# A hybrid decoder layer: the order of convolutions, adaLN tiles and dense tiles around the chunked scan

## What is computed

```python
mod = silu(c) @ w_ada + b_ada                     # adaLN: 12 column tiles of 512
sh1, sc1, g1, sh2, sc2, g2 = split(mod, 6)
h = rmsnorm(x, norm1_g) * (1 + sc1) + sh1
q, k, v, ga, gb, z, xbc, dt = split(h @ w_in)
ya = diff_attention(q, k, v, ...)                 # 8 heads
xbc = silu(causal_depthwise_conv(xbc, conv_w, 4 taps) + conv_b)
xs, bm, cm = split(xbc)                           # 4 groups: xs 512 wide, B and C 128 wide each
y = ssd_chunked(xs * dtp, dtp * a_neg, bm, cm)    # 4 chunks of 128 tokens, a scan over the chunks
y = rmsnorm((y + xs * d_skip) * silu(z))          # per group
merged = sigmoid(ga) * (ya @ w_branch_a) + sigmoid(gb) * (y @ w_branch_b)
x = x + g1 * (merged @ w_out)
x = x + g2 * moe(rmsnorm(x, norm2_g) * (1 + sc2) + sh2)   # 64 experts, top 8, and a shared one
```

## Time and profile before

| | |
|---|---|
| median of three runs | 1998.27 us (1996.91 to 1998.37) |
| the profiled execution, its own time | 1995.61 us |
| its span in the profile | 1993.8 us |
| TensorE busy | 1622.1 us, 81% |
| VectorE busy | 1331.1 us, 67% |
| ScalarE busy | 933.7 us, 47% |
| mean granted TensorE clock over the span | 0.905 |

### The profile page before, as it was taken

How to read it: one execution, slowest core, us unless ns; L and a number is a source line. 1 busy time by engine, 2 the same in 40 slices (tenths; PEclk the granted TensorE clock), 3 DMA queues, 4 the chain that set the end, 5 groups by cost and what they waited for, 6 DMA issues and landing times.

```text
span 1993.8 us, 22702 instructions
## 1 busy us (share of the span) xinstructions
PE 1622.1 (81%) x7242; PEld 1263.5 (63%) x7243; DVE 1331.1 (67%) x1714; ACT 933.7 (47%) x1136; POOL 304.6 (15%) x298
## 2 busy tenths in 40 slices
PE   6697797689798888987878554899999789999960
PEld 1484685567676666765667443687777568877750
DVE  2487467576664656656554674788888457888849
ACT  2325424421324324243233214688887457888740
POOL 1000000011020200201010054222222122222210
PEclk9699899799998989998899776999999889999985
DMA  8021031167211112111142107899999568999948
GB/s 283 22 85 43 22 106 43 71 217 268 99 43 64 43 64 84 43 64 43 42 183 69 43 14 304 324 351 378 359 365 373 199 236 327 373 367 356 347 175 362
DMA packets 103538, 361.43 MB, mean 181 GB/s; under 512 B 19116, under 2 KB 29552, under 8 KB 76432
## 3 DMA queue, kind: packets, MB, share of 16 engines
q1 hardware_dynamic: 71472, 278.41, 37.6%
q0 software_dynamic: 27040, 62.07, 8.5%
q10 hardware_dynamic: 4928, 19.78, 2.5%
HBM read 352.18 MB, written 43.66 MB: 199 GB/s over the span
## 4 chain that ended last, share of the span: by engine, by line
PE 53%; DVE 19%; DMA 14%; ACT 6%; issue 5%; POOL 2%; SPq 0%; ACTq 0%; POOLq 0%; DVEq 0%
PE psum L1279 13%; PE psum L1280 13%; PE psum L1281 13%; DMA rawm<-in_w_exp_up 9%; DVE cv L1804 3%; PE psum L691 2%; DVE ring L850 2%; POOL slot_table L542 2%; ACT hl L1075 2%; PE psum L1301 2%; PE psum L1501 1%; DVE ofin L933 1%; DVE hl L1586 1%; ACT ring L778 1%; DVE modacc L1599 1%
## 5 line engine op out<-in xcount | busy, mean ns | idle before, releaser
L850 DVE TENSOR_TENSOR ring<-rawm,ring 128x2048 fp32r<-128x2048 f32 x192 | 436.3, 2286 | 40.0 <-ACT ring L778 39.4
L778 ACT ACTIVATE ring<-rawm 128x2048 fp32r<-128x2048 f32 x192 | 368.0, 1918 | 92.4 <-DMA rawm<-in_w_exp_up 40.9
L1279 PE MATMUL psum<-ring,xT 128*128 128x512 f32 x528 | 223.9, 424 | 26.2 <-DVE ring L850 21.4
L1586 DVE TENSOR_TENSOR hl<-raw,hl 128x2048 fp32r<-128x2048 f32 x59 | 135.1, 2292 | 137.4 <-ACT hl L1075 136.9
L1281 PE MATMUL psum<-ring,xT 128*128 128x512 f32 x528 | 210.5, 399 | 0.0
L1280 PE MATMUL psum<-ring,xT 128*128 128x512 f32 x528 | 210.4, 398 | 0.0
L1279 PE MATMUL psum<-hl,hT 128*128 128x512 f32 x416 | 164.7, 396 | 15.5 <-DVE hT L1881 11.2
L637 POOL DMA_INDIRECT y_rows<-yb,row_of x64 | 99.5, 1555 | 438.1 <-ACT yb L822 427.8
L1280 PE MATMUL psum<-hl,hT 128*128 128x512 f32 x416 | 163.6, 393 | 0.0
L1281 PE MATMUL psum<-hl,hT 128*128 128x512 f32 x416 | 163.6, 393 | 0.0
L1279 PE MATMUL psum<-hT,hl 128*128 128x512 f32 x320 | 139.3, 435 | 0.0
(11 more groups left out here) (374 smaller groups left out, 3100.3 us busy)
## 6 DMA issues: line engine op xcount, KB each, us to landing
rawm<-in_w_exp_gate SPq DMA_DIRECT2D x64, 1024.0 KB, 12.2
rawm<-in_w_exp_up SPq DMA_DIRECT2D x64, 1024.0 KB, 15.1
rawm<-in_w_exp_down SPq DMA_DIRECT2D x64, 1024.0 KB, 9.8
raw<-in_w_in SPq DMA_DIRECT2D x36, 1024.0 KB, 5.1
modraw<-in_w_ada POOLq DMA_DIRECT2D x16, 1024.0 KB, 5.7
ysum<-y_rows ACTq DMA_DIRECT2D x16, 1024.0 KB, 9.0
raw<-in_w_ada SPq DMA_DIRECT2D x8, 1024.0 KB, 9.4
raw<-in_w_branch_b SPq DMA_DIRECT2D x8, 1024.0 KB, 5.3
```

The source lines that it names most:

```text
L778: A(ring[:, slot, 1, :], rawm[slot][:], ACT.Copy).then_inc(S["m_hi2"], 1)
L850: TT(ring[:, slot, 0, :], rawm[slot][:], ring[:, slot, 1, :].bitcast(F32), ALU.subtract).then_inc(S["m_lo2"], 1)
L1279: M(dst, lhs(0), rhs(0), start=first, stop=False)
L1586: TT(hl[:, slot, 0, :], raw[slot][:], hl[:, slot, 1, :].bitcast(F32), ALU.subtract).then_inc(S["lo_done"], 1)
```

## The change

- **adaLN halves.** `modacc` has two buffers. The matmul `modp` of a tile comes two output tiles after its second half, and `take_mod` (now a step `modt`) three after. The halves start on the same dense tiles, with `bc` of group 0 now ahead of `xs` of group 0; the last four halves stand behind bc 0, bc 1, xs 0 and xs 1.
- **Convolutions.** B and C of group g+1 (q = 4, 5) are convolved behind the second tile of each of the two b bases of group g; for group 0 behind xs 2 and xs 3. Those of xs stand behind z tiles 0 (q = 0), 1 (q = 1, 2) and 2 (q = 3). `yb_hl` no longer lies over `cv` but over `xs_rows` and `lm`; the convolution of B waits instead for the state products of the group before.
- **The opening of the scan.** "rows" is cut in two: "bc" (B, C, decays of chunk 0, `b_rows`, `cbm`) stands ahead of the four z tiles, "xs" (transposes of xs, inputs of chunk 0) behind them.
- **Filling.** For groups 0 to 2: bc 0 behind "xs", bc 1 behind chunk 0, xs 0 behind chunk 1, xs 1 behind chunk 2, nothing behind chunk 3, xs 2 and xs 3 behind "last". `bc` is created ahead of `xs`. For group 3: one tile behind "xs", one behind chunk 1, two behind "last".

The core of the diff (the buffers' moves in SBUF, and the same split of "rows" on POOL and ACT, are left out):

```diff
@@ plan_steps
-    def mod_unit(j, h):
+    later = []
+
+    def mod_unit():
+        j, h = next(late)
...
-        if h == 0 and j > 4:
-            item("modp", j - 1)
         item("modu", j, u=u)
+        if h:
+            later.append([2, "modp", j])
+            later.append([3, "modt", j])
+
+    def out_mod(b, o, mod=True):
+        out(b, o)
+        for x in list(later):
+            x[0] -= 1
+            if x[0] == 0:
+                item(x[1], x[2])
+                later.remove(x)
+        if mod:
+            mod_unit()
...
-    x = xs(0)
-    for o in range(4):
-        out(x, o)
-        mod_unit(*next(late))
-    x = bc(0)
-    out(x, 0)
-    item("modp", 11)
-    out(x, 1)
+    conv = lambda g, *qs: [item("conv", g, q=q) for q in qs]
+    y, x = bc(0), xs(0)
+    for o in range(2):
+        out_mod(y, o)
+    for o in range(4):
+        out_mod(x, o, o < 2)
+        if o >= 2:
+            conv(0, 2 + o)
+    item("modt", 11)
     for g in range(G4):
         z = base("row", ("z", g), halves(w["w_in"], OZ + g * 512), 4)
-        for o, qs in enumerate(((4, 5), (0,), (1, 2), (3,))):
-            for q in qs:
-                item("conv", g, q=q)
+        part = lambda p: item("ssd", g, part=p)
+        part("bc")
+        for o in range(4):
             out(z, o)
+            conv(g, *((0,), (1, 2), (3,), ())[o])
+        part("xs")
         if g < G4 - 1:
-            x, y = xs(g + 1), bc(g + 1)
-            fill = {"rows": (x, 0), 0: (x, 1), 1: (x, 2), 2: (x, 3), 3: (y, 0), "last": (y, 1)}
+            y, x = bc(g + 1), xs(g + 1)
+            fill = {"xs": [(y, 0)], 0: [(y, 1)], 1: [(x, 0)], 2: [(x, 1)], "last": [(x, 2), (x, 3)]}
         else:
             x = base("col", ("gb", 0), halves(w["w_in"], OGB), 4)
-            fill = {"rows": (x, 0), 1: (x, 1), 3: (x, 2), "last": (x, 3)}
-        for part in ("rows", 0, 1, 2, 3, "last", "norm"):
-            item("ssd", g, part=part)
-            if part in fill:
-                out(*fill[part])
+            fill = {"xs": [(x, 0)], 1: [(x, 1)], "last": [(x, 2), (x, 3)]}
...
         for b in range(2):
-            whole(base("branch", ("b", g, b), [[(0, 512, 0, 4, cols(w["w_b"], g * 512, 4, b * 512))]], 4))
+            x = base("branch", ("b", g, b), [[(0, 512, 0, 4, cols(w["w_b"], g * 512, 4, b * 512))]], 4)
+            for o in range(4):
+                out(x, o)
+                if g < G4 - 1 and o == 1:
+                    conv(g + 1, 4 + b)
@@ TensorE
-                    M(bank(7), ones[:], modacc[:], start=True, stop=True).then_inc(S["mod_ps"], 1)
+                    M(bank(7), ones[:], modacc[:, tag % 2], start=True, stop=True).then_inc(S["mod_ps"], 1)
...
-                        else:
-                            pe.wait_ge(S["yT_lo"], HEADS + 4 * g)
                         pe.wait_ge(S["conv_silu"], 6 * g + 2)
...
                         segments(0)
+                    elif s["part"] == "xs":
                         pe.wait_ge(S["conv_silu"], 6 * (g + 1))
@@ VectorE
-                if u["half"] == 0:
-                    take_mod(u["tag"])
+                if u["half"] == 0 and u["tag"] >= 6:
+                    v.wait_ge(S["mod_ps"], u["tag"] - 1)
...
-                        v.wait_ge(S["proj_done"], out_index[("b", g - 1, 1)] + 4)
+                        v.wait_ge(S["ys_ps"], 4 * g)
```

More of the change, by code:

```diff
@@ L86, in __call__ @@
         return t
+CONV = (4, 5, 0, 1, 2, 3)
 def plan_steps(w):
@@ L151, in plan_steps @@
         for o in range(4):
-            out(x, o)
-            mod_unit(*next(late))
+            out_mod(x, o)
     item("spill", 0)
@@ L1005, in _ @@
                     g = s["tag"]
-                    ch = {"rows": 0, 0: 1, 1: 2, 2: 3, 3: 4}.get(s["part"])
+                    ch = {"bc": 0, 0: 1, 1: 2, 2: 3, 3: 4}.get(s["part"])
                     if ch is not None:
@@ L1667, in _ @@
                     mod_rows(s["u"])
+                elif kind == "modt":
+                    take_mod(tag + 1)
                 elif kind == "h":
@@ L1835, in chunk_inputs @@
                            ALU.mult).then_inc(S["m_ready"], 1)
[L1837 to L1838 removed]
+                    if s["part"] == "bc":
                         v.wait_ge(S["cb_ps"], 2 * g + 2)
```

40 lines of the change are left out of this document (21 added, 19 removed).

## The result

| | before | after |
|---|---|---|
| median | 1998.32 us (1996.91 to 2001.42, four runs) | 1971.56 us (1964.36 to 1974.21, four runs) |
| the profiled execution, its own time | 1995.61 us | 1973.67 us |
| its span | 1993.8 us | 1971.9 us |
| ratio of the times | | 0.9865, 95% interval 0.9842 to 0.9887 |

The account below looks back on a forecast made before the run. TensorE was taken as the bound, waiting on VectorE's wrongly ordered queue, with slow clock after waits. Terms -17.5 - 10.5 + 0.3 - 3 = -30.7 gave 1967 us from the 1998.3 median; range 1958 to 1978, with rivals 1956 to 1983.

Parts of the forecast that it names:

- opening of group 0, with the adaLN sums: Start of the mixer: sums -13.5, group 0's opening -5.5, slow clock +1.5; together -17.5 us, between -12 and -20.
- scans and branches, groups 0 to 2: Norm's wait gone, small new waits at chunks and branch tiles: -3.5 us each, -10.5 in all.
- z stages, groups 1 to 3: Wait before xs transposes shrinks, "bc" waits instead: -2 in groups 1 and 2, +2.8 in 3, clock +0.5 each; +0.3 us.
- scan and branch, group 3: Two tiles behind the last state product cover the norm's 2.5, plus some clock: -3 us, between -1.5 and -4.
- adaLN sums: Sums delayed one tile remove waits and slow clock before them, except the first's wait: -13.5 us, weak end -9.
- The three new waits: Opening of group 0: xs 0 waits 1.4, part "bc" 2.6, transposes of xs 0.5; +4.5 us.
- up to 2 us come back; I take half: Scans of groups 0 to 2: gain if the 1.2 GHz stretch around the norm goes, half of up to 2 us.
- two tiles (11.5 us) cover it ... So -6.3: Norm in groups 0 to 2: chunk 3's output follows at once, two tiles cover 7.9 us to scaling; -6.3 us.
- The queues couple: Rival: ACT holds tiles at a Silu, C's convolution comes 2 to 3 us later, z stage moves; +15, 1982 us, 12%.
- The scan becomes VectorE's: Rival: each chunk of groups 0 to 2 pays its split in full, 38 us; slower, 2006 us, 4%.
- The waits only change their names: Rival: each removed wait returns as another in the scan's chain; within 4 us of 1998, 4%.
- The clock holds: Rival: no new wait brings the clock down, branches run at 2.4 GHz from the start; 1961 us, 15%.

Follow-up runs that it names:

- adaLN delay alone: Changed kernel with only the later adaLN sums, two buffers, divided "rows" and opening order `bc` before `xs` kept; otherwise as before the change: 1981.18 us, ratio 0.9921.
- `xs` created first: Against the kernel with "bc" behind z: `xs` created and used ahead of `bc` again in groups 1 to 3; 1972.47 us, ratio 0.9876.
- the second comparison: The changed kernel measured again, unedited, beside the kernel before: 1963.58 us against 1996.37, ratio 0.9838.
- the fastest two: The kernel with "bc" behind z, 1935.67 us, and the same with gate gb's second weight split behind group 3's last z tile, 1930.12 us.
- the kernel with "bc" behind z: Changed kernel with all six convolutions back among the z tiles and part "bc" directly ahead of "xs": 1935.67 us, ratio 0.9718.
- the late split beside "bc" behind z: The kernel with "bc" behind z, with gate gb's second weight split moved behind the last z tile of group 3: 1930.12 us, ratio 0.9668.

## Why the prediction was right, and where its steps were not

The stages of the mixer stretch, from the traces (predicted, then measured in the first profile; a scan runs from the transposes of xs to the first branch matmul). A branch part ends with its last matmul.

| stage | predicted | measured |
|---|---|---|
| opening of group 0, with the adaLN sums | -17.5 | 158.1 to 141.6, -16.5 |
| scans and branches, groups 0 to 2 | -10.5 | 279.5 to 264.0, -15.5 |
| z stages, groups 1 to 3 | +0.3 | 92.7 to 93.5, +0.8 |
| scan and branch, group 3 | -3 | 94.4 to 90.5, -3.9 |
| sum | -30.7 | -35.1 |

**adaLN sums: right in cause, somewhat over-sized.** The waits before the sums went as worked out. The first keeps its wait (1.18, for 1.37 in the earlier trace rows), and two small ones for `take_mod` (0.73 and 0.39) were not foreseen. The term was -13.5, with -9 as the weak end. Taking the delay back cost 10.8 and 11.4 in the opening, and 6.5 and 9.6 in the whole stretch. The -13.8 of "adaLN delay alone" is not a clean measure of it, since that kernel also has `bc` ahead of `xs` in the opening: where the delay is taken back and that order is kept, the 1.85 of the earlier trace rows is gone all the same, and the 2.10 stands as 2.17.

**Opening: number right, reason partly wrong.** The three new waits were 1.25, 2.64 and 0.52, for 1.4, 2.6 and 0.5 worked out. The transposes of xs began at 530.83 instead of about 525: the stretch begins 1.7 us later in this profile, the term was 1 too large, and the rest is a slip of mine, since 545.6 - 17.5 is 528. The wait of 2.64 did bring the clock down, for 3.4 us from 504.84 on, about 1.7 lost, which I had priced at 1.5. But the 6.06 before the transposes of xs, struck out for the moved convolutions, is still 6.07 with the adaLN part alone (opening 143.3), and is gone once the next group's `bc` is created first (136.4); the moved convolutions and "bc" then cost the opening 5.2 (141.6).

**Scans of groups 0 to 2: waits right, the clock under-sized.** The norm's waits went entirely. The middle chunks wait 1.85 and up to 1.24 (1.6 each worked out), the state product behind chunk 3 waits 1.32 (1.2), a branch tile 1.23 in groups 1 and 2 and 0.43 in group 0 (1.2). The term that failed is the last, "up to 2 us come back; I take half": PE's transposes of xs took 2.5 instead of 3.77 us and the norm's 1.91 instead of 3.67 (3.31 in group 2), all at 1.00 now, and the dense tiles behind them gain too. Over the three groups PE stands 7.7 us less, for 7.5 worked out, while its matmuls take 7.8 less, for the 3 that I took. So they gave 5.0 us more than their sum. One wait went up that I hadn't listed: the branch waits 2.28 for `yb_hl` (1.56 to 1.73 before), because the faster transposes end earlier than VectorE's split of them.

**z stages: waits right, reason wrong.** Waits of 2.64 to 2.90 at "bc" (2.6 and 3.0 predicted), 0.51 before xs in groups 1 and 2 (0.5), 5.79 in group 3 (5.9): every wait was met. The clock behind them was under-sized here too: PE's matmuls take 3.0 us more in the three stages, for 1.5 taken. But the sentence that introduced them, "The wait at the transposes of xs ... shrinks to the 0.5 of above", was read as the doing of the moved convolutions, as I wrote in the expectations too. The sum of waits was made for the new list as a whole, so it came out right whichever edit did it. The experiments show that the order of creation had done it, by one split less among the z tiles, and that the convolutions' move with "bc" ahead of z costs 27.1 us. I had even used the split's place in the working ("Group 3 has two splits among the z tiles (gate gb follows)") without asking what the kernel would be with that edit alone.

**Norm: right in sum, wrong in cause.** The step "two tiles (11.5 us) cover it ... So -6.3" gave the second tile the whole. It is worth 2.5; 3.8 came from the split that the order of creation takes away. With `xs` created first the second tile left 3.5 of the 6.3, so it was worth 2.8 there.

**The median.** From the stretch, 1998.3 - 35.1 would be 1963.2; the second comparison gave 1963.58, the first 1971.56, with its experts' part 11.9 longer than in the repeat. The forecast of 1967 lies between them, partly by luck: a gain of the stretch taken 4.4 too small, and an experts' part that was slow in the first comparison.

**The rivals.** *The queues couple* did not happen: "bc" never waits for over 2.90. *The scan becomes VectorE's* did not: no state product in groups 0 to 2 waits over 1.85. *The waits only change their names* held for the convolutions' edit alone, and there more than that. *The clock holds* was half true. Behind the waits at "bc" it fell in groups 0 and 1, and it was at 0.50 around that of group 2 (from 736.95 on), but it stayed at 1.00 behind the 2.90 of group 3. It held through the norm's transposes in groups 0 to 2, and in groups 1 and 2 it fell for 3.4 us behind the wait for `yb_hl` instead (709.64, 829.11). The stretch from 620.90 to 624.30 at 0.50 stands right behind a wait of 2.70, as the one of the earlier trace rows stood behind 2.03. The Trainium skill ("TensorE: Matmul & The Clock Gate", "HAM oscillation — how this bites in real kernels") ties the slow state to long idle gaps; these two rows speak against that. The 5.79 in group 3 doesn't: that long wait had 0.50 around it too (887.13 to 893.96).

## What to carry to other kernels

When a wait goes because a list was reordered, ask for each edit of the list alone which position made it go: the one that the change is named after can be the one that costs. In a ring of weights whose splits hang on "the base before", which base is created next decides how many splits stand in a critical place; here that was worth more than every move of the convolutions. And when a small piece of TensorE's own work is moved ahead, ask what that piece itself waits for there: "bc" behind z never waited, and ahead of z it waited 11.1 us in four groups, while the cover that it had given to the transposes of xs was worth some 0.5 a group.

## What the runs showed of the hardware

**What the waits cost, the clock adds to by about half.** Over all kernels, the same 2,297 matmuls of the mixer stretch took from 521.6 to 544.8 us, and PE busy mostly falls as PE standing falls: between before and the fastest two, 39.0 and 43.4 us less of standing came with 23.2 and 21.9 less of busy. A wait of 2.70 was followed by 3.4 us at 0.50 (620.90 to 624.30, above), and three waits of 2.7 to 2.9 taken away returned 13.6 us, of which 9.6 are standing (with a little at state products and in the branch tiles) and 4.0 are matmuls. That it is the clock can be read from the trace: in before, 74.7 us of PE's busy time in the stretch lie where 0.50 is granted, in the kernel with "bc" behind z 27.1, and half of that difference is 23.8, for the 23.2 measured. As an estimate from this table alone: a microsecond of standing removed brought back about 1.5 (1.4 to 1.6 in these three). Single edits range wider: the adaLN delay taken back cost 6.7 of standing and no slower matmuls, the late split beside "bc" behind z brought 4.4 of standing and 1.4 us of slower matmuls.

**Where the clock falls is not fixed by the kernel.** The same four matmuls in the same place (decays of chunk 0, group 2), first in the one, then in the other execution of the kernel after, behind the same wait of 2.90:

```profile
740.13 2.00 PE L1466 MATMUL psum<-ua,later 128*128 128x512 f32 x4
...
741.13 3.58 PE L1466 MATMUL psum<-ua,later 128*128 128x512 f32 x4
```

In the first the clock was back at 1.00 some 0.2 us after they had started, in the second it stayed at 0.50 until 744.5, for nearly all of their time. Nothing here tells what decides it, and it stays open. The same shows between kernels: the adaLN sums' delay cost 10.8 us in the opening and 6.5 in the whole, and the two scans that differed had the same instructions.

**The experts' part scatters by itself.** With the same instructions it took 778.3 and 790.2 us in two executions of the kernel after, at granted clocks of 0.93 and 0.91, and 779.8 and 782.7 in two of before. That is as much as several of the single edits here are worth: the delay taken back cost 12.2 us by the medians of one session and 6.5 by the stretch. The mixer stretch repeated within 0.2 us, though its parts did not quite (the scan of group 2 took 64.4 and 63.3 us in the two executions of after).
